# A two-layer decoder trunk on one core: neighbouring blocks paired in both MLPs, the passages into and out of their up-projections reordered, and the down projections' weight halves made by two engines

## Chip, core and metric

The kernel runs on one core of a Trainium2 chip. The metric is the device time of one execution in microseconds, as the median of the runs. The core has TensorE (PE in the rows, with PEld for its weight loads), VectorE (DVE), ScalarE (ACT), GpSimd (POOL), and SyncE (SP), which here only issues DMAs. Each engine takes its own instructions in the order in which they were issued, and they wait for each other by semaphores.

## The reference

The input x is 1024 positions by 1024 channels in float32. There are two layers, each a mixer with a residual and then an MLP with a residual:

```python
for layer in range(2):
    x = x + pool_diffattn_layer(x, ...)   # layer 0; layer 1: mlstm_layer(x, ...)
    x = x + conv_ffn(x, ffn_norm_g[layer], ffn_w_up[layer], ffn_conv_w[layer],
                     ffn_conv_b[layer], ffn_w_down[layer])

def conv_ffn(x, norm_g, w_up, conv_w, conv_b, w_down):
    h = causal_depthwise_conv(rms_norm(x, norm_g) @ w_up, conv_w, conv_b)   # width 3
    g, u = jnp.split(h, 2, axis=-1)                                         # 2816 columns each
    return (jax.nn.silu(g) * u) @ w_down
```

The mixers end in a 1024 by 1024 output projection. The change touches the passage from it into the MLP, the MLP, and nothing else.

## The kernel before

**Precision and layout.** Activations lie transposed: `res[:, c, :]` holds channels 128c to 128c+127 (chunk c of KC = 8) by S = 1024 positions. Each float32 factor is split into a high part (rounded to float32r by a copy) and a low part (the rest); a product is three matmuls: high by high, high by low, low by high. A matmul has 128 by 128 weights and 512 moving columns (HALF).

**Output projection (`pe_out`).** Output chunk d is one weight tile and 8 groups (`pe_group`) of 6 matmuls. It fills one half of PSUM `pj`, the halves alternating. `dve_out_add` adds it into `res`. The last two chunks, 6 and 7, are interleaved after the table `LAST_PAIR`, so that the mixer's input buffer falls free early: in the order 6, 6, 7, 7, 6, 7, five groups of 6, five groups of 7. Each further group of chunk 7 adds one to `xa_free`.

**Up-projection.** It is a Strassen-like product: for each of FC = 22 column blocks j, seven products `a11 s2 s3 s1 a22 a12 s4` (for j = 0 in the order `a11 s1 a12 s4 s2 s3 a22`) of 12 matmuls each. Its moving side is, for each pair of chunks p, the plain first half (`a11`) and the difference of halves (`s1`, made by `dve_out_low` through `wsum`) of one chunk, the whole of the other (`a12`, `s4`), and three sums of both (`s2`, `s3`, `a22`; made from the base copy `rbc` of `act_pair_base` by `dve_pair_sums`, split by `act_pair_high` and `dve_pair_low`). Chunk p is paired with chunk p + 4. The weights are summed by GpSimd (`pool_s1` to `pool_s4`), their high parts cut by ScalarE (`act_cut`, in the order of the products), their low parts made by GpSimd (`pool_low`).

**After the products.** `act_p1` copies `a11`'s result out of PSUM, and `a12` may overwrite that bank only then. VectorE combines (`dve_u2`, `u3`, `c22`, `c21`, `c11`, `c12`); inside `dve_c21` and `dve_c12` it multiplies by the row norm (this gives `ffn_hg` and `ffn_hu`). ScalarE starts the convolution in PSUM `dn` (`act_center`), VectorE adds the two other taps (`dve_taps`), ScalarE does SiLU (`act_silu`), VectorE the gating (`dve_gated`). Product `a22` of block j needs `u3` of the same block, since both use one bank. Gated blocks go to DRAM and come back as `act_stage`.

**Norm statistics.** `act_norm_square` squares each chunk, GpSimd adds (`add_squares`), and `pe_stat` sums across partitions between the products of j = 0.

**Down projection (`pe_down`).** There are 22 weight tiles and 22 activation blocks, in six groups of 4, 4, 4, 4, 2, 4. Block p is split by `act_gated_high` and `dve_gated_low`. The first group starts as each of its first four blocks arrives. Output block 0 needs part `c21` of j = 21, block 1 `c12`, block 2 the last SiLU, block 3 the last gated block. The weight tiles are split by GpSimd alone, high part and low part (`pool_cut`, in the rows L1978 and L1980).

The order of the work on each engine is written out by hand in `act_out_norm`, `dve_out`, `dve_ffn`, `act_ffn`, `pool_ffn` and `sp_ffn`.

## Time and profile before

| | |
|---|---|
| time, median of 3 runs | 2207.36 us (2207.21 to 2207.53) |
| profiled execution: its own time | 2207.0 us |
| its span in the trace | 2204.8 us |
| PE busy | 98% of the span |
| DVE / POOL / ACT busy | 60% / 53% / 36% |
| layer 0: last matmul of the output projection to the first of the up-projection | 404 us |
| layer 0: up-projection / down projection | 404 to 849 / 850 to 1094 us |
| layer 1: up-projection / down projection | 1511 to 1955 / 1956 to 2202 us |

The profiled execution took 0.4 us less than the median of the runs. A row's first number is the start, or the busy time, as its group says; "idle before <- X" is how long the engine stood still before the instruction and what ended that. "issue" is a wait that the profile gives to no instruction, often one for several semaphores. A busy PE isn't PE at its peak: neighbouring matmuls overlap, and one starts every 0.23 us though a row gives 0.39 us.

### The profile page before, as it was taken

What the parts mean: (1) busy time and instruction counts of PE and PEld (TensorE: products, weight loads), DVE (VectorE), ACT (ScalarE), POOL (GpSimd) and SP (SyncE); (2) the same over time, 40 slices, a digit from 0 to 9 for tenths busy, and PEclk for the clock granted to TensorE, in tenths of its full rate; (3) what the DMA queues carried; (4) which work ended last, traced back from release to release, by engine and by line L of the source; (5) the groups of instructions that cost most, each with busy time, mean ns of one, the idle gap of its engine ahead of it and who ended that gap; (6) DMA issues with size and microseconds to landing.
All of it is one profiled execution on the core that took longest, in us unless ns stands there. A gap on an engine that the chain in (4) does not pass through costs nothing.

```text
span 2204.8 us, 26660 instructions
## 1 busy us (share of the span) xinstructions
PE 2153.2 (98%) x10219; PEld 1776.0 (81%) x10219; DVE 1328.5 (60%) x1423; ACT 790.2 (36%) x1266; POOL 1179.4 (53%) x708
## 2 busy tenths in 40 slices
PE   9999999799999999999999999997999999999999
PEld 8777778678888887888888898886788888878887
DVE  7776766677777777334544244366677777773342
ACT  6555452444434443000343434424434444430000
POOL 2212216677777775444643333275777777754442
PEclk9999999899999999999999999998999999999999
DMA  6111012022222224222321021030222222243221
GB/s 204 55 49 49 26 46 107 19 77 87 80 83 77 86 87 153 90 91 71 112 82 58 20 77 58 20 143 19 73 81 79 85 86 87 81 144 100 86 67 77
DMA packets 50429, 174.80 MB, mean 79 GB/s; under 512 B 6080, under 2 KB 8192, under 8 KB 50304
## 3 DMA queue, kind: packets, MB, share of 16 engines
q1 hardware_dynamic: 42816, 147.49, 20.2%
q10 hardware_dynamic: 7488, 25.61, 3.2%
q8 instruction: 82, 1.34, 0.2%
q14 instruction: 43, 0.35, 0.1%
HBM read 139.23 MB, written 29.66 MB: 77 GB/s over the span
## 4 chain that ended last, share of the span: by engine, by line
PE 90%; DVE 5%; issue 3%; POOL 2%; ACT 1%; ACTq 0%; DVEq 0%; POOLq 0%
PE pj L1684 36%; PE pj L355 14%; PE dn L1726 11%; PE pj L1726 10%; PE pj L328 6%; PE pj L2231 3%; PE dn L720 1%; PE pj L746 1%; DVE act_lo_buf L1813 1%; POOL ssum L438 1%; PE dn L2370 1%; PE pj L537 1%; PE pj L730 1%; POOL w_lo L1615 1%; PE dn L2379 1%
## 5 line engine op out<-in xcount | busy, mean ns | idle before, releaser
L1978 POOL TENSOR_TENSOR w_hi<-w_raw,ones 128x1024 fp32r<-128x1024 f32 x98 | 190.4, 1943 | 746.9 <-PE pj L328 170.3
L1615 POOL TENSOR_TENSOR w_lo<-w_sum,w_hi 128x512 fp32r<-128x512 f32 x176 | 272.3, 1559 | 122.6 <-ACT w_hi L1609 122.6
L1980 POOL TENSOR_TENSOR w_lo<-w_raw,w_hi 128x1024 fp32r<-128x1024 f32 x98 | 259.0, 2643 | 7.7
L1609 ACT ACTIVATE w_hi<-w_sum 128x512 fp32r<-128x512 f32 x176 | 106.5, 628 | 311.2 <-POOL w_sum L1630 168.9
L1615 POOL TENSOR_TENSOR w_lo<-w_raw,w_hi 128x512 fp32r<-128x512 f32 x132 | 172.6, 1308 | 81.7 <-ACT w_hi L1609 81.7
L1684 PE MATMUL pj<-t_hi,w_hi 128*128 128x512 f32 x520 | 204.7, 394 | 10.0 <-DVE ffn_v L1759 10.0
L1684 PE MATMUL pj<-t_lo,w_hi 128*128 128x512 f32 x520 | 204.2, 393 | 0.0
L1684 PE MATMUL pj<-t_hi,w_lo 128*128 128x512 f32 x520 | 203.8, 392 | 0.0
L1684 PE MATMUL pj<-xb_hi,w_hi 128*128 128x512 f32 x348 | 136.5, 392 | 12.4 <-issue 12.4
L1684 PE MATMUL pj<-xa_hi,w_hi 128*128 128x512 f32 x348 | 136.2, 391 | 12.4 <-issue 12.4
L1850 ACT ACTIVATE act_hi_buf<-act_stage 128x1024 fp32r<-128x1024 f32 x40 | 41.7, 1056 | 293.1 <-PE dn L1726 192.3
L1870 DVE TENSOR_TENSOR res<-dn,res 128x1024 f32<-128x1024 f32 (+1 forms) x49 | 58.9, 1202 | 134.6 <-PE dn L1726 134.6
L1870 DVE TENSOR_TENSOR res<-pj,res 128x1024 f32<-128x1024 f32 x48 | 58.7, 1224 | 134.6 <-PE pj L1726 134.6
L1684 PE MATMUL pj<-xb_lo,w_hi 128*128 128x512 f32 x348 | 136.3, 392 | 0.0
L1684 PE MATMUL pj<-xb_hi,w_lo 128*128 128x512 f32 x348 | 136.2, 392 | 0.0
L1684 PE MATMUL pj<-xa_lo,w_hi 128*128 128x512 f32 x348 | 136.1, 391 | 0.0
L1684 PE MATMUL pj<-xa_hi,w_lo 128*128 128x512 f32 x348 | 136.0, 391 | 0.0
L355 PE MATMUL pj<-xb_hi,w_hi 128*128 128x512 f32 x384 | 128.3, 415 | 0.0
L1684 PEld LDWEIGHTS pj<-t_hi,w_hi 128*128 128x128 f32 x520 | 98.5, 189 | 35.6 <-issue 10.9
L1609 ACT ACTIVATE w_hi<-w_raw 128x512 fp32r<-128x512 f32 x132 | 82.7, 627 | 103.4 <-PE pj L1684 103.4
L355 PE MATMUL pj<-xb_lo,w_hi 128*128 128x512 f32 x384 | 119.1, 392 | 0.0
L1726 PE MATMUL pj<-act_hi_buf,w_hi 128*128 128x512 f32 x352 | 109.4, 392 | 9.7 <-DVE act_lo_buf L1813 6.2
(378 smaller groups left out, 5459.1 us busy)
## 6 DMA issues: line engine op xcount, KB each, us to landing
w_raw<-weights SPq DMA_DIRECT2D x187, 512.0 KB, 3.5
gated_rows<-ffn_gated SPq DMA_DIRECT2D x40, 512.0 KB, 2.6
act_stage<-gated_rows ACTq DMA_DIRECT2D x32, 512.0 KB, 3.3
x_first<-x_t SPq DMA_DIRECT2D x8, 512.0 KB, 7.5
res<-x_t SPq DMA_DIRECT2D x8, 512.0 KB, 6.7
act_stage<-gated_rows SPq DMA_DIRECT2D x8, 512.0 KB, 5.0
scratch<-res ACTq DMA_DIRECT2D x8, 512.0 KB, 2.6
res<-scratch SPq DMA_DIRECT2D x8, 512.0 KB, 7.3
```

The costliest lines, as they stand in the source:

```text
L328: ins = pe.matmul(o, w, x[:, k, t * HALF:(t + 1) * HALF], start=(k == 0 and m == 0), stop=(k == KC - 1 and m == 2))
L355: ins = pe.matmul(o[:, t * HALF:(t + 1) * HALF], w, x[:, k, t * HALF:(t + 1) * HALF], start=(first and m == 0), stop=(last and m == 2))
L438: eng.tensor_tensor(ssum[:, :], ssum[:, :], squares_of(ph, c)[:, :], ALU.add).then_inc(norm_acc[ph], 1)
L1609: act.activation(f.cut(t, whi), f.source(j, name), ACT.Copy).then_inc(c_high, 1)
L1615: pool.tensor_tensor(f.cut(t, wlo), f.source(j, name), f.cut(t, whi).bitcast(F32), ALU.subtract).then_inc(c_ready, 1)
L1684: ins = pe.matmul(o, f.cut(t, w)[:, k * P:(k + 1) * P], f.moving(name, x, k), start=(not more and k == 0 and q == 0), stop=(k == KC // 2 - ...
L1726: ins = pe.matmul(f.room(e)[:, t * HALF:(t + 1) * HALF], w[:, wsl, at0:at0 + P], x[:, p % SLOTS, t * HALF:(t + 1) * HALF], start=(i == 0 a ...
L1850: act.activation(f.hi[:, p % SLOTS, :], f.gated_source(p), ACT.Copy).then_inc(act_hi, 1)
L1870: dve.tensor_tensor(res[:, d, half], f.room(e)[:, half], res[:, d, half], ALU.add).then_inc(down_added, 1)
L1978: pool.tensor_tensor(whi[:, w, :], raw[:, r, :], ones[:, 0:1].to_broadcast([P, D]), ALU.mult).then_inc(w_high, 1)
L1980: pool.tensor_tensor(wlo[:, w, :], raw[:, r, :], whi[:, w, :].bitcast(F32), ALU.subtract).then_inc(w_ready, 1)
L2231: ins = pe.matmul(value_bank(h, b), XB[mine][:, x, b * P:(b + 1) * P], theirs[:, wsl, w], start=(t == 0 and k == 0 and q == 0 and b % 2 == 0),
```

## The change

- **Pairing.** Chunk 2p is now paired with chunk 2p + 1. Even chunks give `a11` and `s1`, odd ones `a12` and `s4`. The weights are laid out accordingly on the host.
- **Sums during the output projection.** `dve_pair_sums` of pairs 0 and 1 run after chunks 1 and 3, into spare parts of the near buffer (chunks 6 and 7 of X); pair 2's also go there, only pair 3's in the far buffer. So chunk 6 is written after the low parts of pairs 0 and 1, chunk 7 after pair 2's.
- **`LAST_PAIR`**: chunk 7 gets its group 3 before chunk 6's last four.
- **Queues of the passage.** `act_p1` of j = 0 moves ahead of the last two cuts and the last pair's high part. GpSimd makes `s1`, `s2`, `s3` of j = 0 ahead of the sum of squares.
- **Block 0 to 1.** `dve_u2` and `dve_u3` of j = 1 move ahead of the second taps of j = 0; ScalarE does both `act_center` of j = 0 at once.
- **Last block.** The multiplications by the row norm leave `dve_c21` and `dve_c12`; for j = 21 they run after the low parts of the first four gated blocks. ScalarE makes the four high parts in a row.
- **Down weights.** ScalarE copies the high part (`act_down_high`), GpSimd only the low part (`pool_down_low`), in 22 tiles of each layer.

```diff
         def act_out_norm(act, l):
             for c in range(KC - 2):
                 act_out_chunk(act, f, c)
-            act_pair_base(act, f, 0)
+                if c % 2:
+                    act_pair_base(act, f, c // 2)
             act_cut(act, f, 0)
-            act_pair_base(act, f, 1)
+            act_cut(act, f, 1)
             act_pair_high(act, f, 0)
-            act_cut(act, f, 1)
-            act_pair_base(act, f, 2)
             act_pair_high(act, f, 1)
             act_out_chunk(act, f, KC - 2)
             act_cut(act, f, 2)
+            act_pair_high(act, f, 2)
             act_pair_base(act, f, 3)
-            act_pair_high(act, f, 2)
+            act_cut(act, f, 3)
             act_out_chunk(act, f, KC - 1)
-            act_cut(act, f, 3)
+            act_p1(act, f, 0)
             act_cut(act, f, 4)
+            act_cut(act, f, 5)
             act_pair_high(act, f, 3)
-            act_cut(act, f, 5)
...
         def dve_out(dve, l):
             for d in range(KC - 2):
                 dve_out_add(dve, l, d)
                 dve_out_low(dve, f, d)
-            dve_pair_sums(dve, f, 0)
-            dve_pair_sums(dve, f, 1)
+                if d in (1, 3):
+                    dve_pair_sums(dve, f, d // 2)
             dve_pair_low(dve, f, 0)
+            dve_pair_low(dve, f, 1)
+            dve_pair_sums(dve, f, 2)
             dve_out_add(dve, l, KC - 2)
-            dve_pair_low(dve, f, 1)
             dve_out_low(dve, f, KC - 2)
-            dve_pair_sums(dve, f, 2)
+            dve_pair_low(dve, f, 2)
             dve_out_add(dve, l, KC - 1)
-            dve_pair_low(dve, f, 2)
+            dve_pair_sums(dve, f, 3)
             dve_out_low(dve, f, KC - 1)
-            dve_pair_sums(dve, f, 3)
             dve_pair_low(dve, f, 3)
...
+        def act_down_high(act, f, n):
+            if n < f.T1 + W_RING:
+                act.wait_ge(prod_done, f.l * N_PROD * FC + N_PROD * FC - 4 + 2 * (n - f.T1))
+            else:
+                act.wait_ge(tile_done, td(n - W_RING + 1))
+            raw_landed(act, n)
+            act.activation(whi[:, n % W_RING, :], raw[:, n % RAW_RING, :], ACT.Copy).then_inc(w_high, 1)
+        def pool_down_low(pool, n):
+            pool.wait_ge(w_high, td(n + 1))
+            pool.tensor_tensor(wlo[:, n % W_RING, :], raw[:, n % RAW_RING, :], whi[:, n % W_RING, :].bitcast(F32),
+                               ALU.subtract).then_inc(w_ready, 1)
...
             for p in range(4, FC):
                 act_gated_high(act, f, p)
                 act_next_stage(act, f, p)
+                act_down_high(act, f, f.T1 + p - 1)
+            act_down_high(act, f, f.T1 + FC - 1)
```

Three places of the queues follow. Before and after each is layer 0.

ScalarE, the passage into the up-projection, before: `xb_hi` is chunk 7's high part, `t_hi` the last pair's, `ffn_v_0` is `act_p1`, `w_hi` are cuts.

```order
L413 ACTIVATE xb_hi<-res,params 128x1024
L426 ACTIVATE sq_tmp<-res 128x1024
L1609 ACTIVATE w_hi<-w_sum_118 128x512
L1609 ACTIVATE w_hi<-w_sum_119 128x512
L1395 ACTIVATE t_hi_122<-t_sums_124 128x1536
L1609 ACTIVATE w_hi<-w_sum_120 128x512
L1819 ACTIVATE ffn_v_0_126<-pj 128x512
L1609 ACTIVATE w_hi<-w_raw 128x512
```

The same place on ScalarE in the change:

```order
L1631 ACTIVATE w_hi<-w_sum_118 128x512
L413 ACTIVATE xb_hi<-res,params 128x1024
L426 ACTIVATE sq_tmp<-res 128x1024
L1845 ACTIVATE ffn_v_0_130<-pj 128x512
L1631 ACTIVATE w_hi<-w_sum_119 128x512
L1631 ACTIVATE w_hi<-w_sum_120 128x512
L1402 ACTIVATE t_hi_122<-t_sums_last_124 128x1536
L1631 ACTIVATE w_hi<-w_raw 128x512
```

`act_p1` stands right behind chunk 7's square instead of behind the last pair, and the cut of `s4` (source `w_sum_118`) stands ahead of chunk 7.

VectorE, end of block j = 0 and start of j = 1, before: `ffn_v_0` is `u2`, `ffn_v_1` is `u3`, `dn` are taps, `ffn_gated` the gating.

```order
L1800 SCALAR_TENSOR_TENSOR dn<-ffn_hg_125,params,dn 128x1022
L1802 SCALAR_TENSOR_TENSOR dn<-ffn_hg_125,params,dn 128x1023
L1800 SCALAR_TENSOR_TENSOR dn<-ffn_hu_128,params,dn 128x1022
L1802 SCALAR_TENSOR_TENSOR dn<-ffn_hu_128,params,dn 128x1023
L1809 TENSOR_TENSOR ffn_gated_0_130<-ffn_silu_129,dn 128x1024
L1754 TENSOR_TENSOR ffn_v_0_126<-pj,ffn_v_0_126 128x512
L1759 TENSOR_TENSOR ffn_v_1_127<-pj,ffn_v_0_126 128x512
L1767 TENSOR_TENSOR ffn_hg_125<-pj,ffn_v_1_127 128x512
```

The same place on VectorE in the change:

```order
L1826 SCALAR_TENSOR_TENSOR dn<-ffn_hg_129,params,dn 128x1022
L1828 SCALAR_TENSOR_TENSOR dn<-ffn_hg_129,params,dn 128x1023
L1776 TENSOR_TENSOR ffn_v_0_130<-pj,ffn_v_0_130 128x512
L1781 TENSOR_TENSOR ffn_v_1_131<-pj,ffn_v_0_130 128x512
L1826 SCALAR_TENSOR_TENSOR dn<-ffn_hu_132,params,dn 128x1022
L1828 SCALAR_TENSOR_TENSOR dn<-ffn_hu_132,params,dn 128x1023
L1835 TENSOR_TENSOR ffn_gated_0_134<-ffn_silu_133,dn 128x1024
L1789 TENSOR_TENSOR ffn_hg_129<-pj,ffn_v_1_131 128x512
```

`u2` and `u3` have passed the second pair of taps and the gating.

VectorE, the last block j = 21, before: `act_lo_buf` are the low parts of gated blocks for the down projection.

```order
L1776 TENSOR_TENSOR ffn_hg_125<-ffn_hg_125,rms_bc 128x1024
L1813 TENSOR_TENSOR act_lo_buf_133<-ffn_gated_0_130,act_hi_buf_132 128x1024
L1785 TENSOR_TENSOR ffn_hu_128<-pj,rms_bc 128x512
L1813 TENSOR_TENSOR act_lo_buf_133<-act_stage_134,act_hi_buf_132 128x1024
L1789 TENSOR_TENSOR ffn_hu_128<-pj,ffn_v_0_126 128x512
L1794 TENSOR_TENSOR ffn_hu_128<-ffn_hu_128,rms_bc 128x512
L1813 TENSOR_TENSOR act_lo_buf_133<-act_stage_134,act_hi_buf_132 128x1024
L1800 SCALAR_TENSOR_TENSOR dn<-ffn_hg_125,params,dn 128x1022
L1802 SCALAR_TENSOR_TENSOR dn<-ffn_hg_125,params,dn 128x1023
L1813 TENSOR_TENSOR act_lo_buf_133<-act_stage_134,act_hi_buf_132 128x1024
```

The same place on VectorE in the change:

```order
L1839 TENSOR_TENSOR act_lo_buf_137<-ffn_gated_0_134,act_hi_buf_136 128x1024
L1809 TENSOR_TENSOR ffn_hu_132<-pj,rms_bc 128x512
L1839 TENSOR_TENSOR act_lo_buf_137<-act_stage_138,act_hi_buf_136 128x1024
L1813 TENSOR_TENSOR ffn_hu_132<-pj,ffn_v_0_130 128x512
L1839 TENSOR_TENSOR act_lo_buf_137<-act_stage_138,act_hi_buf_136 128x1024 x2
L1800 TENSOR_TENSOR ffn_hg_129<-ffn_hg_129,rms_bc 128x1024
L1820 TENSOR_TENSOR ffn_hu_132<-ffn_hu_132,rms_bc 128x512
L1826 SCALAR_TENSOR_TENSOR dn<-ffn_hg_129,params,dn 128x1022
```

The four low parts now stand ahead of both multiplications by `rms_bc` and ahead of the taps.

## Rows read from the trace of the kernel before

**Rows 1.** Page, busy time, share of the span and instructions of each engine.

```profile
PE 2153.2 (98%) x10219; PEld 1776.0 (81%) x10219; DVE 1328.5 (60%) x1423; ACT 790.2 (36%) x1266; POOL 1179.4 (53%) x708
```

**Rows 2.** Waits of PE: line, for whom, us in total, times, longest us.

```profile
PE pj L1684 <- issue: 24.9, 2, 12.4
PE pj L1684 <- DVE ffn_v L1759: 10.0, 2, 5.0
PE pj L1726 <- DVE act_lo_buf L1813: 6.2, 4, 2.0
PE pj L1726 <- issue: 3.5, 2, 1.8
```

**Rows 3.** Windows: length, PE, PEld, DVE, ACT, POOL busy, PEclk, DMA share, GB/s.

```profile
422.00:428.00 6.00, 5.85 (x15) 4.66 (x16) 0.84 (x1) 0.57 (x2) 3.21 (x2) 0.57 0.27 83
...
1969.00:1975.00 6.00, 6.00 (x21) 4.74 (x20) 5.87 (x5) 2.01 (x2) 2.05 (x2) 0.72 0.35 130
...
876.00:1093.00 217.00, 217.00 (x959) 179.72 (x959) 89.31 (x66) 28.58 (x28) 100.98 (x43) 1.00 0.28 94
```

**Rows 4.** Timeline of PE, layer 0, blocks 0 and 1: start, us, idle before.

```profile
422.15 0.77 PE L1684 MATMUL pj<-xb_hi,w_hi 128*128 128x512 f32 x1 [12.43 <-issue]
...
427.32 0.39 PE L1684 MATMUL dn<-xb_hi,w_hi 128*128 128x512 f32 x1
...
430.04 1.95 PE L373 MATMUL dn<-ones,ssum 128*128 128x128 f32 x16
...
456.98 0.76 PE L1684 MATMUL pj<-t_hi,w_hi 128*128 128x512 f32 x1 [5.02 <-DVE ffn_v L1759]
```

**Rows 5.** Timeline of ACT in the same stretch.

```profile
419.56 1.48 ACT L1395 ACTIVATE t_hi<-t_sums 128x1536 fp32r<-128x1536 f32 x1 [6.08 <-DVE t_sums L1456]
...
421.47 0.58 ACT L1819 ACTIVATE ffn_v<-pj 128x512 f32<-128x512 f32 x1
...
446.55 1.28 ACT L1834 ACT_TABLE_LOAD   x1
...
451.41 0.58 ACT L1819 ACTIVATE ffn_v<-pj 128x512 f32<-128x512 f32 x1
```

**Rows 6.** Timeline of POOL: sums of squares, and one low part of weights.

```profile
386.06 2.62 POOL L438 TENSOR_TENSOR ssum<-ssum,sq_tmp 128x1024 f32<-128x1024 f32 x1 [6.64 <-ACT sq_tmp L426]
...
401.63 3.37 POOL L438 TENSOR_TENSOR ssum<-ssum,sq_tmp 128x1024 f32<-128x1024 f32 x1
...
434.22 1.28 POOL L1615 TENSOR_TENSOR w_lo<-w_raw,w_hi 128x512 fp32r<-128x512 f32 x1 [9.01 <-ACT w_hi L1609]
```

**Rows 7.** Timeline of DVE: pair sums, chunk 6 added, pair sums again.

```profile
392.56 0.74 DVE L1451 SCALAR_TENSOR_TENSOR t_sums<-res,params,rms_bc 128x512 f32<-128x512 f32 x1
...
397.58 1.23 DVE L1423 TENSOR_TENSOR res<-pj,res 128x1024 f32<-128x1024 f32 x1 [1.10 <-PE pj L355]
...
402.67 2.88 DVE L1451 SCALAR_TENSOR_TENSOR t_sums<-res,params,rms_bc 128x512 f32<-128x512 f32 x1
```

**Rows 8.** Timeline of PE at the start of layer 0's down projection.

```profile
853.26 0.70 PE L1726 MATMUL pj<-act_hi_buf,w_hi 128*128 128x512 f32 x2 [1.76 <-issue]
...
862.32 0.73 PE L1726 MATMUL pj<-act_hi_buf,w_hi 128*128 128x512 f32 x2 [1.97 <-DVE act_lo_buf L1813]
```

**Rows 9.** Timeline of DVE there: two low parts of gated blocks.

```profile
846.31 3.42 DVE L1813 TENSOR_TENSOR act_lo_buf<-ffn_gated,act_hi_buf 128x1024 fp32r<-128x1024 f32 x1
...
855.27 1.21 DVE L1813 TENSOR_TENSOR act_lo_buf<-act_stage,act_hi_buf 128x1024 fp32r<-128x1024 f32 x1
```

**Rows 10.** Timeline of POOL there: a low part of down weights.

```profile
845.38 3.26 POOL L1980 TENSOR_TENSOR w_lo<-w_raw,w_hi 128x1024 fp32r<-128x1024 f32 x1
```

**Rows 11.** Page, groups: busy us, mean ns of one, idle before.

```profile
L1615 POOL TENSOR_TENSOR w_lo<-w_sum,w_hi 128x512 fp32r<-128x512 f32 x176 | 272.3, 1559 | 122.6 <-ACT w_hi L1609 122.6
L1980 POOL TENSOR_TENSOR w_lo<-w_raw,w_hi 128x1024 fp32r<-128x1024 f32 x98 | 259.0, 2643 | 7.7
...
L1850 ACT ACTIVATE act_hi_buf<-act_stage 128x1024 fp32r<-128x1024 f32 x40 | 41.7, 1056 | 293.1 <-PE dn L1726 192.3
```

167 lines of the change are left out of this document (103 added, 64 removed).

## The prediction

> **What bounds the kernel now.** First the page's busy times: PE is busy for 98% of the span, the others for 60% or less [rows 1]. So time can only come from PE's gaps, or from matmuls at a lower clock. The list of PE's waits shows where the gaps are [rows 2]: 24.9 us in two waits at L1684 (products, 12.4 us in each layer), 10.0 us in two at L1684 for `u3` (5.0 each), and 6.2 + 3.5 = 9.7 us in six waits at L1726, the start of the down projections. All else PE waits for is under 4 us. In the timeline of PE the first is product `a12` of block 0, the second `a22` of block 1 [rows 4]; the third are the first matmuls of the down projection [rows 8]. The steady part of the down projection has no gap (217.0 of 217.0 us busy [rows 3]), so a cheaper weight cut gains nothing there.
>
> **Clock.** Behind the two longer gaps matmuls are slow. In the steady window 959 start in 217.0 us, one per 0.226 us, at a granted clock of 1.00 (the 2.4 GHz level). The 12 matmuls of `a12` take 427.32 - 422.15 = 5.17 us instead of 2.72: that is the 1.2 GHz level for all of it (the window's mean is 0.57) [rows 3, 4], 2.4 us lost. I allow 1.8 us for `a22`, which starts after 5.02 us of idling. After the shorter gaps of the down projection (2.0 us at most) the clock stayed up in layer 0, but in layer 1 it fell: 0.72 in a window of 6.0 us, (1 - 0.72) x 6.0 = 1.7 us [rows 2, 3].
>
> **First gap, block 0.** `a12` waits for three things: its weights, chunk 7 of X, and `act_p1`. The profile names none ("issue"). `act_p1` ends at 421.47 + 0.58 = 422.05 and `a12` starts at 422.15, so it is `act_p1`. It stands behind the last pair's high part, which itself had waited 6.08 us for VectorE's sums [rows 4, 5]. The change puts it behind chunk 7's square. What is then late? I follow the new queue in the clock of layer 0.
>
> - Chunk 6 now ends one group later. A group is 6 x 0.226 = 1.36 us, so its add (397.58 [rows 7]) starts at 398.94 and ends at 400.17. Difference, high halves and square on ScalarE and VectorE take about 2.4 us more: square done at 402.6.
> - GpSimd then makes sum of squares, low part of `a12`, and `s4`. Alone that is 2.62 + 1.28 + 1.28 = 5.2 us, beside a busy VectorE 3.37 + 1.56 + 1.56 = 6.5 us [rows 6, 11], with a row of the worst some 1 us more. ScalarE has now the cut of `s4` ahead of chunk 7, so this wait holds chunk 7 up: cut done 408.4 to 410.1.
> - Chunk 7's high part, its square and `act_p1` follow, 1.1 + 1.0 + 0.6 = 2.7 us with the starts overlapping a little [rows 5, 11]. `a12` starts between 411.2 and 412.9. I take 412.2, in the upper half, since VectorE works on `pair_low` and sums then. PE began the last of `s1` 12.6 us before 422.15, near 409.6 (its idle time and one step of 0.23), so a gap of 2.6 us remains instead of 12.4.
> - Its last three matmuls need chunk 7's low part. VectorE has ahead of it the sums of pair 3: three instructions at 0.74 alone, up to 2.88 beside GpSimd [rows 7]. That puts the low part at 411.8 to 417.4; I take 415.4, some 1.3 us of further gap.
> - `a12` then ends at 416.1, `s4` at 418.8 (416.6 to 420.8). Before, `s4` ended at 430.04 [rows 4]. Gain 11.2 us (9.2 to 13.4), the slow matmuls' 2.4 us included.
> - Will the clock fall after 2.6 + 1.3 us? Between cases that did (5.0, 12.4) and one layer of two that did at 2.0. I take half of 2.4: **gain 10.0 us in each layer**, bounds 6.8 and 13.4.
>
> Pair sums 0 and 1 now run during the output projection. VectorE has 10.9 us per chunk there and gets some 8 us for an even chunk and 10 for an odd one. PSUM alternates, so it may be a whole chunk late before PE waits: cost nothing. It would cost something from an average of 10.9 us.
>
> **Second gap, block 1.** `u3` of block 1 stood behind the second taps and the gating, and ended just before it. Now it stands before them, but `u2` needs `act_p1` of block 1, which ScalarE makes behind `act_silu`, and that needs the first taps and its table (load at 446.55, 1.28 us). One `act_center` more (1.2 us) now precedes the load and one fewer follows. `act_p1` moves only from 451.41 to 450.8 [rows 5]; then 0.6 + 0.7 + 0.7 us and `a22` can start at 453.0 instead of 456.98 [rows 4]: 4.0 us, and the 1.8 us of slow matmuls with it, as 1.2 us of idling remain. But VectorE has the taps and the gating still to do (3.9 us) and so begins block 1's `c21` 1.7 us late. Its round has little slack (in the last block `u3` ended 0.3 us before PE wanted it; the timeline there is not among the rows), so `a22` of block 2 waits 0.9 to 1.5 us. **Gain 4.6 us in each layer**, bounds 2.3 (clock still falls) and 5.8 (no wait in block 2).
>
> **Third gap, start of the down projection.** There VectorE's four low parts stood among a multiplication, taps, and waits for ScalarE. Now they come first, each followed only by the combination that frees a PSUM bank. Times here are again layer 0's, from the timeline of that stretch, of which the rows give the ends. Block 0's high part is ready at 844.45 as before, the others at 1.06 us each [rows 11], with a down weight's high part of 1.06 us in between: 846.5, 847.5, 848.5. The low parts end near 845.8, 849.4, 851.3 and 852.5, and `c12` at 850.1. PE finishes the products at 848.6 and uses a block each 2.7 us: only 0.2 us is left to wait, or 0.7 if the first low part takes 3.42 us as in [rows 9]. What is late next is the last SiLU, which output block 2 needs at 859.7: multiplication 1.3, centre 1.2, taps 2.6, SiLU 1.0, so ready at 858.8, 0.9 us before; beside GpSimd the multiplication alone takes 1 us more. I leave 0.4 us. Gain 9.7 / 2 - 0.4 = 4.5 in layer 0, and 4.5 + 1.3 = 5.8 in layer 1 where the clock had fallen: **10.3 us in both**, bounds 5 and 12.
>
> A page of the Trainium skill bears on this, "SBUF — State Buffer", section "Who interferes with whom": a VectorE instruction with two SBUF inputs and a GpSimd one that reads SBUF lock each other out whole, and the later one waits. The row agrees: the low part of 3.42 us began inside GpSimd's, which ended at 848.64, and ended 1.1 us after that, where another took 1.21 us [rows 9, 10]. By that rule the first low part, at 844.5 now ahead of GpSimd's start at 845.6, takes 1.2 us and the gain is 0.5 us per layer more than by the row of 3.42.
>
> **Down weights on ScalarE.** 44 copies of 1.06 us on an engine busy for 36% [rows 1, 11], GpSimd keeps its 2.64 us. Behind each copy ScalarE queues the next gated block's high part. A copy may start when tile n - 3 is done, and its 1.1 + 2.6 us lie under two tiles of 10.9 us each. Cost nothing; if the cover went, 3.7 us per tile at most.
>
> **Sum.** 2 x 10.0 + 2 x 4.6 + 10.3 = 39.5 us. The profiled execution would go from 2207.0 to 2167.5 us (span 2165.3, with 2.2 us around it). The median is 0.4 us above it: **2167.9 us**, 1.8% faster. With all lower bounds, 2 x 6.8 + 2 x 2.3 + 5 = 23.2 us, 2184; with all upper ones 2 x 13.4 + 2 x 5.8 + 12 = 50.4 us, 2157.
>
> **Rivals.**
>
> - *The work is in a cheaper order than I draw it*: no clock fall after the first gap, chunk 7's low part early, no wait in block 2. Then 2 x 12.5 + 2 x 5.8 + 11 = 47.6 us, 2160. For it: many of my durations are those beside GpSimd. Against: GpSimd is busy just then.
> - *The gap moves to chunk 7's chain*: GpSimd's sum of squares, `s4`, the cut, chunk 7, `act_p1` are one chain now, and the clock falls at both places. Gain 2 x 7 + 2 x 2.8 + 8 = 27.6 us, 2180. For it: every step there has a row that is longer under contention [rows 6, 7].
> - *Slower: ScalarE's queue in the down projections.* A weight's copy stands behind a gated-block DMA issue that waits for VectorE's low part, which waits for PE's output block. If it came so late that the tile's low part ended after PE was done with the tile before, PE would stop once per tile. It decides from 18 us of delay, 21.8 - 3.7. At 2 us in each of 19 tiles of two layers: +76 - 39.5, 2244. Against: by my reading VectorE's low part p + 1 comes before the tile's end for which the copy waits anyway.
> - *It does nothing*: `a12` really waited for chunk 7 or weights. Then only the other gaps go, 20 us, 2187. Against: the end of `act_p1` and the start of `a12` meet within 0.1 us [rows 4, 5], and in both layers alike [rows 2].
>
> **Chances.** Forecast (31 to 45 us) 0.60; cheaper order 0.15; moved gap (22 to 31 us) 0.13; `act_p1` not the cause 0.03; slower 0.04; something small that cancels nearly all 0.02, the rest between these. About 0.2% (4.4 us) is what a measurement of this kernel can tell from no change. Faster 0.94, same 0.02, slower 0.04. The range, 2157 to 2182, leaves out the slower case and the ends of the others.
>
> **What will show it.** `a12`'s idle at 2 to 4 us instead of 12.4, its releaser `act_p1` or chunk 7's low part; `s4` ended 11 us sooner after the output projection. `a22` of block 1 idle for 1 us, with a wait of 1 us in block 2. The six waits at L1726 nearly gone. POOL's busy time down by its 44 copies, ACT's up by 44 x 1.06 = 47 us, PE's window of the down projection unchanged. I am wrong if the output projection shows gaps, if PE waits at each weight tile, or if the clock's slow matmuls take over what the gaps gave.

## The result, and the profile after

The changed kernel takes **2169.16 us** (median of 4 runs, 2168.22 to 2173.05) against 2207.28 us for the kernel before on the same chip: the ratio is 0.9831, with a 95% interval from 0.9814 to 0.9848. The forecast was 2167.9 us. The profiled execution took 2168.6 us.

The page, busy times of the engines, to be read against [rows 1]:

```profile
span 2166.8 us, 26682 instructions
...
PE 2146.3 (99%) x10219; PEld 1771.1 (82%) x10219; DVE 1330.1 (61%) x1425; ACT 832.1 (38%) x1312; POOL 1075.4 (50%) x664
```

PE has the same 10219 matmuls and is busy 7 us less, since fewer of them run at the lower clock. POOL lost its 44 instructions and 104 us, ACT has 46 more and 42 us. The span fell by 2204.8 - 2166.8 = 38.0 us.

The waits of PE in the kernel after (line, for whom, us in total, times, longest us), against [rows 2]:

```profile
PE pj L1706 <- DVE ffn_v L1781: 7.6, 4, 2.5
PE pj L1706 <- POOL w_lo L1637: 2.6, 1, 2.6
PE pj L1706 <- issue: 2.6, 1, 2.6
```

L1706 is the products' line now, L1748 that of the down projection. Nothing waits at L1748 any more, where there were six waits. The first gap is 2.6 us in each layer instead of 12.4 (the profile gives it to "issue" in one layer and to a low part of weights in the other), and two waits for `u3` in each layer stand where there was one. The timeline of PE, layer 0:

```profile
412.70 0.76 PE L1706 MATMUL pj<-xb_hi,w_hi 128*128 128x512 f32 x1 [2.59 <-issue]
...
417.06 0.40 PE L1706 MATMUL dn<-xb_hi,w_hi 128*128 128x512 f32 x1
...
419.80 1.95 PE L373 MATMUL dn<-ones,ssum 128*128 128x128 f32 x16
...
442.96 0.47 PE L1706 MATMUL pj<-t_hi,w_hi 128*128 128x512 f32 x1 [1.23 <-DVE ffn_v L1781]
...
464.79 0.47 PE L1706 MATMUL pj<-t_hi,w_hi 128*128 128x512 f32 x1 [2.54 <-DVE ffn_v L1781]
...
835.60 0.62 PE L1748 MATMUL pj<-act_hi_buf,w_hi 128*128 128x512 f32 x2
```

These are `a12` and `s4` of block 0, the statistic, `a22` of block 1, `a22` of block 2, and the first matmul of the down projection. Two stretches make comparison easy. **U** runs from the first product's first matmul to the first one of the down projection. Before it took 445.77 us in layer 0 and 444.67 in layer 1, after it 431.09 and 430.92. **M** runs from the start of the first down projection to the first product of layer 1: 661.56 us before, 657.50 after.

On ScalarE the row that the forecast was about, and three rows of block 1 that matter below (timeline of ACT, kernel after):

```profile
409.51 0.63 ACT L1631 ACTIVATE w_hi<-w_sum 128x512 fp32r<-128x512 f32 x1 [3.47 <-POOL w_sum L1664]
...
412.03 0.58 ACT L1845 ACTIVATE ffn_v<-pj 128x512 f32<-128x512 f32 x1
...
450.43 1.16 ACT L1631 ACTIVATE w_hi<-w_sum 128x512 fp32r<-128x512 f32 x2 [3.70 <-POOL w_sum L1659]
451.49 0.61 ACT L1631 ACTIVATE w_hi<-w_raw 128x512 fp32r<-128x512 f32 x1
452.01 1.19 ACT L1854 ACTIVATE dn<-ffn_hg,params 128x1024 f32<-128x1024 f32 x1
```

`act_p1` (L1845) ends at 412.61, and `a12` starts at 412.70. What holds `act_p1` back is the cut of `s4` at 409.51, which waited 3.47 us for GpSimd's sum, with chunk 7's high part and square between.

### The profile page after: what moved, and what is told of

The parts are those of the page before. It is cut to its first block and busy times, and to the rows that moved or that the text cites. A ratio compares the mean times of both kernels' runs of the same rounds, so it can differ in the third digit from the quotient of the medians.

```text
span 2166.8 us, 26682 instructions
## 1 busy us (share of the span) xinstructions
PE 2146.3 (99%) x10219; PEld 1771.1 (82%) x10219; DVE 1330.1 (61%) x1425; ACT 832.1 (38%) x1312; POOL 1075.4 (50%) x664
## 5 line engine op out<-in xcount | busy, mean ns | idle before, releaser
L2039 POOL TENSOR_TENSOR w_hi<-w_raw,ones 128x1024 fp32r<-128x1024 f32 x54 | 105.8, 1959 | 494.3 <-PE pj L328 170.3
L1637 POOL TENSOR_TENSOR w_lo<-w_sum,w_hi 128x512 fp32r<-128x512 f32 x176 | 274.2, 1570 | 103.0 <-ACT w_hi L1631 103.0
L1896 POOL TENSOR_TENSOR w_lo<-w_raw,w_hi 128x1024 fp32r<-128x1024 f32 x44 | 105.9, 2407 | 342.1 <-ACT w_hi L1891 342.1
L1706 PE MATMUL pj<-t_hi,w_hi 128*128 128x512 f32 x520 | 203.1, 391 | 7.6 <-DVE ffn_v L1781 7.6
L1637 POOL TENSOR_TENSOR w_lo<-w_raw,w_hi 128x512 fp32r<-128x512 f32 x132 | 172.7, 1309 | 64.1 <-ACT w_hi L1631 64.1
L1706 PE MATMUL pj<-t_hi,w_lo 128*128 128x512 f32 x520 | 202.8, 390 | 0.0
L1706 PE MATMUL pj<-t_lo,w_hi 128*128 128x512 f32 x520 | 202.7, 390 | 0.0
L1891 ACT ACTIVATE w_hi<-w_raw 128x1024 fp32r<-128x1024 f32 x44 | 46.6, 1059 | 317.6 <-PE dn L1748 168.7
L1706 PE MATMUL pj<-xb_hi,w_hi 128*128 128x512 f32 x348 | 136.3, 392 | 2.6 <-issue 2.6
L1706 PE MATMUL pj<-xa_hi,w_hi 128*128 128x512 f32 x348 | 136.2, 391 | 2.6 <-POOL w_lo L1637 2.6
L2041 POOL TENSOR_TENSOR w_lo<-w_raw,w_hi 128x1024 fp32r<-128x1024 f32 x54 | 135.1, 2502 | 4.2
L1706 PE MATMUL pj<-xa_lo,w_hi 128*128 128x512 f32 x348 | 136.1, 391 | 0.0
L1706 PE MATMUL pj<-xa_hi,w_lo 128*128 128x512 f32 x348 | 135.9, 391 | 0.0
L1706 PE MATMUL pj<-xb_lo,w_hi 128*128 128x512 f32 x348 | 135.9, 391 | 0.0
L1706 PE MATMUL pj<-xb_hi,w_lo 128*128 128x512 f32 x348 | 135.9, 391 | 0.0
L1839 DVE TENSOR_TENSOR act_lo_buf<-act_stage,act_hi_buf 128x1024 fp32r<-128x1024 f32 x40 | 80.2, 2008 | 80.0 <-ACT act_hi_buf L1876 80.0
L1706 PEld LDWEIGHTS pj<-t_hi,w_hi 128*128 128x128 f32 x520 | 97.6, 188 | 33.5 <-issue 6.3
L355 PE MATMUL pj<-xb_hi,w_lo 128*128 128x512 f32 x384 | 118.5, 390 | 0.0
```

The source lines that it names most:

```text
L355: ins = pe.matmul(o[:, t * HALF:(t + 1) * HALF], w, x[:, k, t * HALF:(t + 1) * HALF], start=(first and m == 0), stop=(last and m == 2))
L1637: pool.tensor_tensor(f.cut(t, wlo), f.source(j, name), f.cut(t, whi).bitcast(F32), ALU.subtract).then_inc(c_ready, 1)
L1706: ins = pe.matmul(o, f.cut(t, w)[:, k * P:(k + 1) * P], f.moving(name, x, k), start=(not more and k == 0 and q == 0), stop=(k == KC // 2 - ...
L1839: dve.tensor_tensor(f.lo[:, p % SLOTS, :], f.gated_source(p), f.hi[:, p % SLOTS, :].bitcast(F32), ALU.subtract).then_inc(act_lo, 1)
L1891: act.activation(whi[:, n % W_RING, :], raw[:, n % RAW_RING, :], ACT.Copy).then_inc(w_high, 1)
L1896: pool.tensor_tensor(wlo[:, n % W_RING, :], raw[:, n % RAW_RING, :], whi[:, n % W_RING, :].bitcast(F32), ALU.subtract).then_inc(w_ready, 1)
```

## The experiments

Each time is compared with runs of the kernel before on the same chip (their medians lie between 2206.36 and 2207.49 us). Five of the runs split the change's gain, seven look for what is left.

### The first gap: `act_p1` put back (x1_p1_back)

```diff
 # act_out_norm of the kernel after
             act_out_chunk(act, f, KC - 1)
-            act_p1(act, f, 0)
             act_cut(act, f, 4)
             act_cut(act, f, 5)
             act_pair_high(act, f, 3)
+            act_p1(act, f, 0)
```

> The changed kernel with act_p1 of block 0 moved back behind the last cuts and the last pair's high part; all else as changed. Theory A (act_p1 frees the bank and its place in ScalarE's queue sets when a12 starts): the last high part ends at 415.0 in the changed trace, so act_p1 ends near 416.1 and a12 starts 3.4 us later in each layer (idle about 6 us instead of 2.6, matmuls behind it slow again), 2169 + 7 = 2176 us. Rival (chunk 7's low part, ready at 416.2, sets it anyway): the gap grows, but a12's last three matmuls waited until then already, so less than 2 us in all.

Measured: 2175.45 us (2175.13 to 2176.21), ratio 0.9857 [0.9842, 0.9872]. Waits of PE in this kernel:

```profile
PE pj L1706 <- issue: 10.0, 2, 5.0
PE pj L1706 <- DVE ffn_v L1781: 7.5, 4, 2.5
```

One instruction behind three others costs 6.3 us. The gap is 5.0 us and not the 6 expected, since `act_p1` ends at 414.81; `a12` starts at 414.91, 0.1 us behind it, as it does in the kernels before and after. The block waits don't move.

### The first gap: only `act_p1` moved, in the kernel before (x2_p1_on_before)

```diff
 # kernel before: act_out_norm
             act_out_chunk(act, f, KC - 1)
+            act_p1(act, f, 0)
             act_cut(act, f, 3)
 # act_ffn
-            act_p1(act, f, 0)
             act_cut(act, f, 2 * W_RING)
```

> The kernel before with one edit: act_p1 of block 0 stands right behind chunk 7's square. Pairing, sums and all other orders as before. Theory A (the first gap was mostly the queue position of act_p1): a12 starts when chunk 7's low part is there, 413.5 instead of 422.15 in layer 0's clock, and the last pair's low part (422.8) is then just in time for s2's last matmuls: 8.7 + up to 2.4 us of slow matmuls per layer, 2207 - 17 to 22 = 2185 to 2190 us. Rival (the pairing and the sums during the output projection carry the first gap's 10.6 us): the wait moves to s2, whose sums are as late as before, and less than 10 us are won in all, 2197 us or more.

Measured: 2188.53 us (2188.05 to 2189.76), ratio 0.9917 [0.9902, 0.9931]. Waits of PE:

```profile
PE pj L1685 <- DVE ffn_v L1760: 10.0, 2, 5.0
PE pj L1685 <- issue: 6.7, 2, 3.3
PE pj L1727 <- DVE act_lo_buf L1814: 6.2, 4, 2.0
PE pj L1727 <- issue: 3.5, 2, 1.8
```

This moved line alone gives 19 us, half of the whole change. The gap falls from 12.4 to 3.3 us, where the whole change has 2.6; the other waits stay as in [rows 2]. From the first product to the statistic it is 16.1 and 17.2 us in the two layers, 15.3 and 15.4 in the kernel after: so the rest of the passage's changes (the pairing with its sums during the output projection, `LAST_PAIR`, the order of the other work) is worth 0.8 and 1.8 us on top, and part of the 1.8 is the clock, as layer 1 of this run has 14 slow matmuls behind the gap and layer 0 has 9. The rest pays in another way: with the old position of `act_p1` the new kernel waits 5.0 us where the old one waited 12.4. No run takes the pairing apart from the other orders.

### The first gap: `act_p1` still earlier (x10_passage)

```diff
 # kernel after: act_out_norm
+            act_p1(act, f, 0)
             act_cut(act, f, 3)
             act_out_chunk(act, f, KC - 1)
-            act_p1(act, f, 0)
 # dve_out
-            dve_pair_sums(dve, f, 3)
             dve_out_low(dve, f, KC - 1)
+            dve_pair_sums(dve, f, 3)
```

> After, with ScalarE's reading of the first block's product ahead of the cut of its last weight, and VectorE's last low part of the normalised input ahead of the last pair of sums. If the 2.6 us left at the first gap are ScalarE standing behind that cut (which waited 3.47 us for GpSimd's sum), the gap at 412.7 falls to 0 to 0.5 us in each layer, 4 to 5 us in all; if the clock then does not fall, another 1.5 us a layer comes with it: 2161 to 2165 us. If the last sum is late for its weight, a new wait of up to 1.5 us a layer stands behind the low part of the paired input: 2166 to 2168 us.

Measured: 2170.07 us (2168.53 to 2170.25), ratio 0.9833 [0.9820, 0.9846]: no change, and above both expectations. The timeline of PE says where the 2.6 us went:

```profile
412.50 0.47 PE L1706 MATMUL pj<-xb_hi,w_hi 128*128 128x512 f32 x1 [0.60 <-DVE xb_lo L1450]
421.90 0.50 PE L1706 MATMUL pj<-t_hi,w_hi 128*128 128x512 f32 x1 [1.92 <-DVE t_lo L1476]
```

`a12` now starts with no gap and only its last three matmuls wait 0.6 us. But the last pair's sums begin 2.9 us later on VectorE and their low part is late for `s2`, 1.9 us in each layer: the risk named beforehand. From the first product to the statistic this kernel takes 11.7 us, 3.6 less than the kernel after, and all of it is lost again behind the statistic. Block 1's wait rose too in layer 0 (2.10 us; it is 0.71 in layer 1). So the cause of the gap is right, and this cure hands it on.

### The third gap: only the weights' high parts on ScalarE (x4_weights_on_before)

```diff
 # kernel before: act_ffn, pool_ffn
+                act_down_high(act, f, f.T1 + p - 1)
...
-                pool_cut(pool, n, n, 16 * (n // RAW_RING + 1))
+                pool_down_low(pool, n)
```

> The kernel before with ScalarE making the high parts of the down weights and GpSimd the low parts, nothing else changed. Theory A: the first low part is no longer held for 3.4 us behind GpSimd's, so 0 to 4 us in all are won, all at the start of the down projections, and the other waits there (for the last low part behind the taps) stay: 2203 to 2207 us. Rival (ScalarE's queue becomes late in the steady part): waits at each tile, above 2207 us.

Measured: 2204.23 us (2202.87 to 2205.47), ratio 0.9986 [0.9976, 0.9995]. Waits of PE at the down projection:

```profile
PE pj L1726 <- DVE act_lo_buf L1813: 4.5, 2, 2.3
PE pj L1726 <- issue: 0.8, 2, 0.4
```

5.3 us of waits instead of 9.7, so 4.4 us less. Of these 1.2 us come back as slow matmuls, since the clock now falls behind the last wait in layer 0, where it had stayed up (0.83 from 856 to 866 us, against 1.00 from 858 to 868 in the kernel before). ScalarE's 44 copies cost nothing that shows, and GpSimd's 102 us less of work bring 3 us.

### The third gap: the weights back on GpSimd (x3_weights_back)

The same edit undone in the kernel after.

> The changed kernel with the down projections' weights split by GpSimd alone again, both parts. Theory A (the steady down projection has no gap, the cheaper cut gains only at its start, where GpSimd's longer work locks VectorE out of its low parts): 0.3 to 3 us per layer slower, in waits at the start of the down projections, steady part unchanged: 2170 to 2175 us. Rival (the start is carried by VectorE's new order alone): within 1 us of the changed kernel.

Measured: 2177.35 us (2174.92 to 2178.58), ratio 0.9864 [0.9849, 0.9879]: 8.2 us, more than expected. Timeline of PE in this kernel, then of DVE, then of POOL:

```profile
848.78 0.98 PE L1748 MATMUL dn<-act_hi_buf,w_hi 128*128 128x512 f32 x2 [1.86 <-issue]
```

```profile
836.96 5.64 DVE L1839 TENSOR_TENSOR act_lo_buf<-act_stage,act_hi_buf 128x1024 fp32r<-128x1024 f32 x2
842.53 1.21 DVE L1800 TENSOR_TENSOR ffn_hg<-ffn_hg,rms_bc 128x1024 f32<-128x1024 f32 x1
```

```profile
835.55 2.64 POOL L2032 TENSOR_TENSOR w_hi<-w_raw,ones 128x1024 fp32r<-128x1024 f32 x1 [0.20 <-PE pj L1706]
838.27 3.26 POOL L2034 TENSOR_TENSOR w_lo<-w_raw,w_hi 128x1024 fp32r<-128x1024 f32 x1
```

And the same place in the kernel after (timeline of DVE):

```profile
831.51 1.23 DVE L1839 TENSOR_TENSOR act_lo_buf<-ffn_gated,act_hi_buf 128x1024 fp32r<-128x1024 f32 x1 [0.46 <-ACT act_hi_buf L1876]
...
836.61 2.34 DVE L1839 TENSOR_TENSOR act_lo_buf<-act_stage,act_hi_buf 128x1024 fp32r<-128x1024 f32 x2
```

Two low parts take 5.64 us beside GpSimd's two instructions and 2.34 us when GpSimd rests. The 3.3 us go through the multiplication, the centre term and the taps into the last SiLU, which output block 2 awaits: 1.86 us of wait, and the first matmuls behind it are slow (0.98 us for two, 0.62 else). M grows by 661.78 - 657.50 = 4.3 us, of which this wait is 1.9, a shorter one at the start 0.3, and the slow matmuls, by the starts of their rows, 1.7. So in waits the move is worth the same in both orders, 4.4 us in the old one and 2 x (1.86 + 0.3) = 4.3 in the new one. In time it is worth 3 us in the old order and 8 in the new one, and the difference is the clock: here each layer's long wait brings slow matmuls that the kernel after has none of, while in the old order the move leaves waits of 2.3 us and their slow matmuls in place.

### The third gap: the last block's old order (x8_last_back)

```diff
 # kernel after: dve_ffn, last block
             dve_c21(dve, f, j)
+            dve_hg(dve, f, j)
             dve_gated_low(dve, f, 0)
             dve_c11(dve, f, j)
             dve_gated_low(dve, f, 1)
             dve_c12(dve, f, j)
+            dve_hu(dve, f, j)
             dve_gated_low(dve, f, 2)
-            dve_gated_low(dve, f, 3)
-            dve_hg(dve, f, j)
-            dve_hu(dve, f, j)
             dve_taps(dve, f, j, 0)
+            dve_gated_low(dve, f, 3)
             dve_taps(dve, f, j, 1)
 # act_ffn: the centre term between the high parts again
```

> After, with the last block's order on VectorE and ScalarE as it was before (multiplication of the gate half ahead of the low parts, centre term between the high parts), and the high parts of the down weights left on ScalarE. If the order carries the rest of the third gap, PE waits again at the start of the down projection as in the run with the weights alone, 2.3 to 2.7 us a layer, and with slow matmuls behind it 5 to 7 us in all: 2174 to 2176 us. If moving the weights' high parts was enough once the rest of the kernel is changed: 2169 us.

Measured: 2176.27 us (2176.07 to 2176.99), ratio 0.9860 [0.9843, 0.9876]. The waits at L1748 are 4.5 and 0.8 us, the very numbers of the run with the weights alone:

```profile
PE pj L1748 <- DVE act_lo_buf L1839: 4.5, 2, 2.3
PE pj L1748 <- issue: 0.8, 2, 0.4
```

The third gap was 9.7 us of waits. The weights take away 4.4, the order the other 5.3. The time grew by more, 7.1 us; 2.2 us of it lie in U of layer 0 (433.3 us against 431.1), where the clock also fell behind block 2's wait in the profiled execution, far from the edit.

### Block 2's wait: GpSimd sooner (x6_cut_first)

```diff
 # kernel after: act_ffn
             act_cut(act, f, 2 * W_RING)
+            act_cut(act, f, N_PROD)
             act_stat_factors(act, ph)
-            act_cut(act, f, N_PROD)
```

> After, with the high part of the normalised input's last chunk made ahead of the statistic's factors on ScalarE, so that GpSimd can begin block 1's sums some 2.7 us sooner (it idled 2.68 us for this high part at 423.98). GpSimd theory (block 2's first matmul waits 2.54 us because GpSimd is late with the sums that ScalarE's block 1 cuts need): that wait falls to 0 to 0.5 us in each layer, 2164 to 2165 us. VectorE theory (VectorE's own work of block 1 is too long, as the prediction had it): the wait stays 2.5 us, 2169 us. ScalarE's queue order theory: the wait shrinks only by as much as the cuts come sooner.

Measured: 2170.89 us (2167.8 to 2171.2), ratio 0.9835 [0.9822, 0.9849], and block 2's wait is 2.51 us in both layers. GpSimd does begin block 1's sums 3.2 us sooner (422.01 instead of 425.22), but 18 us later only 0.5 us of that are left (440.33, against 440.81): it waits again for ScalarE's cuts. Its late start isn't the cause. In layer 0 the clock stayed up behind the first gap here, and chunk 7's low part now holds up `a12` (timeline of PE):

```profile
415.82 0.47 PE L1706 MATMUL pj<-xb_hi,w_hi 128*128 128x512 f32 x1 [1.05 <-DVE xb_lo L1450]
```

### Block 2's wait: the first centre term ahead of the cuts (x7_center_first)

```diff
 # kernel after: act_ffn, j = 1
+                    if j == 1 and i == 4:
+                        act_center(act, f, j, 0)
...
                     if i == 6:
-                        if j < FC - 1:
+                        if 1 < j < FC - 1:
                             act_center(act, f, j, 0)
```

> After, with the centre term of block 1's first half put on ScalarE ahead of the last cuts of block 2's sums instead of behind them. ScalarE's queue theory (the centre term at 452.0 stood behind cuts that waited 3.70 us for GpSimd's sum, and VectorE's taps waited 3.45 us for it): block 2's wait of 2.54 us goes to 0 to 0.3 us in each layer, with everything else in place, 2164 to 2165 us. VectorE theory: the wait stays at 2.5 us, 2169 us; if the cuts that now come later are themselves needed at once, a new wait of up to 1.2 us a layer stands on the low or high part of a weight.

Measured: 2169.84 us (2169.02 to 2171.93), ratio 0.9835 [0.9821, 0.9848]: no gain, and block 2's wait is 3.0 us instead of 2.5. Timeline of ACT, then of DVE:

```profile
448.77 1.21 ACT L1854 ACTIVATE dn<-ffn_hg,params 128x1024 f32<-128x1024 f32 x1 [2.49 <-DVE ffn_hg L1800]
...
457.56 0.63 ACT L1631 ACTIVATE w_hi<-w_sum 128x512 fp32r<-128x512 f32 x1 [3.87 <-POOL w_sum L1664]
458.10 1.19 ACT L1854 ACTIVATE dn<-ffn_hu,params 128x1024 f32<-128x1024 f32 x1
459.23 0.58 ACT L1845 ACTIVATE ffn_v<-pj 128x512 f32<-128x512 f32 x1
```

```profile
450.01 1.29 DVE L1826 SCALAR_TENSOR_TENSOR dn<-ffn_hg,params,dn 128x1022 f32<-128x1022 f32 x1 [0.68 <-ACT dn L1854]
...
459.32 1.29 DVE L1826 SCALAR_TENSOR_TENSOR dn<-ffn_hu,params,dn 128x1022 f32<-128x1022 f32 x1 [4.26 <-ACT dn L1854]
```

The first centre term came 3.2 us sooner and the first taps with it. VectorE then stood still for 4.26 us, since the second centre term (458.10) was behind the cut of the next `s4`, which waited 3.87 us for GpSimd. The theory of ScalarE's queue was right in kind; I had named one of two places.

### Block 1's wait: its `act_p1` ahead of the SiLU (x9_p1_of_1)

```diff
 # kernel after: act_ffn
                     if i == 0:
+                        if j == 1:
+                            act_p1(act, f, j)
                         act_silu(act, f, j - 1)
                     if i == 1:
                         if j > 1:
                             act_center(act, f, j - 1, 1)
-                        act_p1(act, f, j)
+                            act_p1(act, f, j)
```

> After, with the plain product of block 1 read by ScalarE ahead of block 0's SiLU (and its table load). If block 1's accumulator is held by its first reader on ScalarE, block 1's wait of 1.23 us in each layer goes to 0, and the time falls by 2.5 us to 2166.7 us. If it is held by VectorE's reading of the other accumulator, nothing moves: 2169 us. If the SiLU, later by 0.6 us, holds up block 2, block 2's wait of 2.54 us grows by as much and the sum stays within 1 us of 2169.

Measured: 2170.26 us (2169.57 to 2170.47), ratio 0.9835 [0.9822, 0.9849]. Block 1's wait is gone, but the time isn't better. Block 2's wait is 3.2 us, and slow matmuls follow it (timeline of PE, then of DVE):

```profile
463.86 0.55 PE L1706 MATMUL pj<-t_hi,w_hi 128*128 128x512 f32 x1 [3.23 <-DVE ffn_v L1781]
464.21 0.63 PE L1706 MATMUL pj<-t_lo,w_hi 128*128 128x512 f32 x1
```

```profile
444.35 0.69 DVE L1794 TENSOR_TENSOR ffn_hg<-pj,ffn_v 128x512 f32<-128x512 f32 x1 [0.29 <-PE pj L1706]
...
452.31 1.28 DVE L1826 SCALAR_TENSOR_TENSOR dn<-ffn_hg,params,dn 128x1022 f32<-128x1022 f32 x1 [4.55 <-ACT dn L1854]
```

So the two block waits are largely one delay paid in two places. Counted from the start of `a12`, `a22` of block 2 begins at 51.4 us here and at 52.1 in the kernel after (layer 0): of the 1.2 us won in block 1, 0.7 are left, and the slow matmuls behind the longer wait take those. VectorE isn't late any more at block 1's `c21` (the first row, where it waits for PE), and block 2 waits all the same, because VectorE then stands still for 4.55 us for the centre term.

### All of ScalarE's queue of blocks 1 and 2 (x13_blocks)

The edits of the last two runs together, and for j = 2 the second centre term and `act_p1` ahead of the cut at i = 1:

```diff
+                    if j == 2 and i == 1:
+                        act_center(act, f, 1, 1)
+                        act_p1(act, f, 2)
```

> After, with ScalarE's queue of blocks 1 and 2 rearranged as one piece: block 1's plain product read ahead of block 0's SiLU, block 1's first centre term ahead of the cuts of block 2's sums, and its second centre term and block 2's plain product ahead of the cut that waits for GpSimd's next sum. Each of these alone only handed the wait on (from block 1 to block 2, or from the first centre term to the second). If ScalarE's queue is the whole cause, u3(2) ends about 459.4 us against its matmul at 460.5 and both block waits go to 0, 3.7 us a layer, 7.4 us of PE's waits and about 1 us of slow matmuls behind them: 2161 to 2163 us. If GpSimd's sums are the bound behind it, some 2 us a layer stay as a wait on the low part of a weight: 2165 to 2167 us. If VectorE's work itself is, 2168 to 2170 us.

Measured: 2165.7 us (2164.3 to 2165.96), ratio 0.9811 [0.9796, 0.9826]. No wait in blocks 1 and 2 is left. VectorE's `u3` of block 2 starts at 459.16 and is done before `s1` ends. But block 3 now waits, which none of the three expectations had:

```profile
PE pj L1706 <- DVE ffn_v L1781: 4.1, 2, 2.1
```

7.6 us of waits became 4.1.

### The passage as well (x12_both)

```diff
 # added to the run above; act_out_norm
+            act_p1(act, f, 0)
+            act_norm_high(act, 2 * l + 1, KC - 1, f.X, res[:, KC - 1, :], ready, value)
             act_cut(act, f, 3)
-            act_out_chunk(act, f, KC - 1)
-            act_p1(act, f, 0)
+            act_norm_square(act, 2 * l + 1, KC - 1, res[:, KC - 1, :])
 # dve_out
-            dve_pair_sums(dve, f, 3)
+            dve_pair_sums(dve, f, 3, (0,))
             dve_out_low(dve, f, KC - 1)
+            dve_pair_sums(dve, f, 3, (1, 2))
```

and `act_cut(act, f, N_PROD)` moved as in the run x6_cut_first. `dve_pair_sums` does the steps that its last argument names, `ready` and `value` are the wait of `act_out_chunk`.

> The kernel of the blocks run with the passage rearranged too: ScalarE reads the first block's product, then makes chunk 7's high part, then the cut that waits for GpSimd; VectorE makes chunk 7's low part between the first and the second operation of the last pair sums; and the cut of block 1's plain product stands ahead of the statistic's factors. If the 2.6 us at the first gap are ScalarE's queue alone, they go to 0 to 0.5 us in each layer and the slow matmuls behind them (1.5 us) go too, with up to 1 us a layer of a new wait for the last pair's low part: 2154 to 2159 us. If, as with the simpler rearrangement, the wait is handed on to the last pair's low part (1.9 us a layer) in full, the gain over the blocks run is under 2 us.

Measured: 2161.52 us (2159.24 to 2162.39), ratio 0.9792 [0.9777, 0.9806], 2.5 us above the expected range, as block 3 still waits 2.0 to 2.2 us with slow matmuls behind. The first gap has shrunk to 0.4 us behind the last pair's low part (waits of PE):

```profile
PE pj L1710 <- DVE ffn_v L1785: 4.2, 2, 2.2
...
PE pj L1710 <- DVE t_lo L1479: 0.8, 2, 0.4
```

From the first product to the statistic it is 11.52 us in both layers, 15.3 and 15.4 in the kernel after and 25.9 and 25.3 before.

### Every block (x14_all_blocks)

```diff
 # act_ffn of the run above
-                    if j == 1 and i == 4:
+                    if i == 4 and j < FC - 1:
                         act_center(act, f, j, 0)
-                    if j == 2 and i == 1:
-                        act_center(act, f, 1, 1)
-                        act_p1(act, f, 2)
+                    if i == 1 and j > 1:
+                        act_center(act, f, j - 1, 1)
+                        act_p1(act, f, j)
...
-                    if i == 1 and j > 2:
-                        act_center(act, f, j - 1, 1)
-                        act_p1(act, f, j)
-                    if i == 6:
-                        if 1 < j < FC - 1:
-                            act_center(act, f, j, 0)
```

> The kernel with blocks and passage rearranged, with the order of ScalarE's queue that blocks 1 and 2 have now in every block: the first centre term ahead of the cuts of the next block's sums, the second one and the next plain product ahead of the cut that waits for GpSimd's next sum. In the run before it the wait had moved to block 3 (2.1 to 2.2 us in each layer at 479.03, with 1 us of slow matmuls behind it), where the centre term stood behind cuts again (idle 3.70 on ScalarE, 3.45 on VectorE). If that queue is the cause there too, the wait goes: 2155 to 2158 us. If VectorE and GpSimd lag behind TensorE from the passage on for another reason, the wait goes on to block 4 and the time stays at 2160 to 2162 us. If cuts that now stand behind a centre term are late in the steady blocks, new waits on the low part of a weight make it slower than 2162 us.

Measured: **2154.05 us** (2153.72 to 2154.21), ratio 0.9759 [0.9746, 0.9773], slightly better than the best expectation. It beats both kernels: 15 us below the kernel after, 53 below the one before. Waits of PE at the products, all that is left, and a window (PE busy, then PEld, DVE, ACT, POOL, clock, DMA share, GB/s):

```profile
PE pj L1710 <- DVE t_lo L1479: 0.8, 2, 0.4
```

```profile
430.00:480.00 50.00, 50.00 (x222) 41.31 (x221) 38.70 (x36) 23.98 (x33) 42.57 (x32) 1.00 0.29 95
```

That window was 46.23 us busy in the kernel after. U is 423.64 and 423.83 us, and the mean clock of the execution is 1.000 (0.998 after, 0.991 before). Against the run before it, the 4.2 us of waits gave 7.5 us: by the starts of the rows, the other 3.3 us are slow matmuls that stood behind them.

## Why the prediction came out right, point by point

The time was 1.3 us off, and the sum of 39.5 us stands against 38.0 measured in the span. The terms, with the first gap as the way from the first product to the statistic, the second as the rest of U without its last wait, and the third as that wait (1.11 us) with what lies behind:

| term | forecast, both layers | measured |
|---|---|---|
| first gap | 20.0 | 10.64 + 9.95 = 20.6 |
| second gap | 9.2 | 2.93 + 2.69 = 5.6 |
| third gap | 10.3 | 5.17 + 7.02 = 12.2 |
| output projection of layer 0 | 0 | -0.4 |
| sum | 39.5 | 38.0 |

(Third gap: 1.11 + 661.56 - 657.50, and 1.11 + 5.91, where 5.91 is how much shorter the end of the span is behind the second start. The output projection's -0.4 is scatter: the first product starts between 404.02 and 404.54 us over all the kernels.)

That the sum is nearer than its terms is luck: the errors are +0.6, -3.6, +1.9 and -0.4 us and offset each other.

- **First gap: right, the gap itself by its own working.** Forecast: `a12` at 412.2 with a gap of 2.6 us; it started at 412.70 with 2.59, and 0.4 of the 0.5 us lies in the output projection, which ended later by that. The chain named (GpSimd's sum, the cut of `s4`, chunk 7, `act_p1`) is the one in the rows, and x1 and x2 show that the place of `act_p1` carries it. The last steps are right in their sum only. Chunk 7's low part ended at 416.16, even later than forecast (415.4), and still cost nothing, because the clock fell in both layers: `a12` took 417.06 - 412.70 = 4.36 us for 12 matmuls instead of 2.72, and its last three, which need the low part, came at 416.35 anyway. The forecast added 1.3 us for the wait and 1.2 for half a clock fall, but the slow matmuls run through the wait. Where the clock stayed up behind this gap (layer 1 of x3, layer 0 of x6, layer 1 of x13), PE did wait 1.05 to 1.09 us for that low part, and from the first product to the statistic these take 15.1 us, against 15.3 and 15.4 in the kernel after: here the fall cost 0.2 to 0.3 us net. So the end of `s4`, 419.80 against 418.8 + 1.2 = 420.0, came out right with two wrong parts in it.
- **Second gap: the term that was mis-sized, for a wrong cause.** Block 1 was right (wait 1.23 us, 1.2 forecast, no slow matmuls). Block 2 waited 2.54 us and not 0.9 to 1.5, so 5.6 us came of 9.2: per layer 5.02 - 1.23 - 2.54 = 1.25 us of idling and the slow matmuls behind the old gap. The step that failed is "But VectorE has the taps and the gating still to do (3.9 us) and so begins block 1's `c21` 1.7 us late" as the reason for block 2's wait. The lateness came, but VectorE stood idle behind it for longer, 3.45 us for the centre term at 452.01, which stood behind two cuts that waited for GpSimd (the row below, timeline of DVE). I had worked out VectorE's load and never followed ScalarE's queue through block 1. x13 shows it: with VectorE's work untouched and only ScalarE's order changed, both waits go, and x14 removes block 3's in the same way. That the gain itself comes from `u2` and `u3` standing ahead of the second taps is read from the rows; no run put them back.

```profile
453.23 1.29 DVE L1826 SCALAR_TENSOR_TENSOR dn<-ffn_hg,params,dn 128x1022 f32<-128x1022 f32 x1 [3.45 <-ACT dn L1854]
```

- **Third gap: gone, more than forecast.** The wait of 0.4 us and the late SiLU didn't come (SiLU ended at 845.04, its output block starts near 846.5). The forecast had "0.2 us is left to wait, or 0.7 if the first low part takes 3.42 us as in [rows 9]": it took 1.23 us (831.51 above). This is what the rule of the Trainium skill gave ("SBUF — State Buffer", "Who interferes with whom": a VectorE instruction with two SBUF inputs and a GpSimd one that reads SBUF contend for one pair of ports, which is an exclusive lock). The trace agrees: VectorE's began at 831.51, and GpSimd's only at 832.51. The rows of x3 agree once more: 5.64 us for two low parts, behind and between GpSimd's. The term of layer 1 was also too small by its own rows: the clock's fall there is worked out as 1.7 us ([rows 3]) and then enters the sum as 1.3.
- **Down weights on ScalarE.** "Cost nothing" is right: no gap in the steady projection (216.00 of 216.00 us busy from 860 to 1076), and no wait at a weight tile. The rival of a slower kernel is thereby out. But I counted no gain for it by itself either, only as part of the third gap, and by x3 it carries 8 us there, slow matmuls included. ScalarE's busy time rose by 42 us and not by 47.
- **Rivals.** "It does nothing" fell with x1 and x2. "The gap moves to chunk 7's chain" is true of the place and not of the size. "A cheaper order" needed no clock fall and no wait in block 2, and both came.

What stays open: x10's 2.10 us of block 1's wait in one layer and 0.71 in the other weren't followed up, nor which of the rearrangements in x12 is worth how much of its 4 us, nor what the pairing alone is worth.

## What to carry to other kernels

An in-order engine that serves two chains should be read as a queue, and each instruction that others wait for should stand ahead of the ones that themselves wait: 19 us came of one moved line, and 15 more of ScalarE's order with a split of VectorE's sums. A wait that is handed on isn't a refuted cause: two cures that each gained nothing (x7, x9) gave 3.5 us together with a third place of the same queue, and 7.5 more when every block had it. Where a short gap is left, price it with the matmuls behind it, which often run at half the clock for a while. But don't add that price to a second wait that stands right behind the gap, as this prediction did: the slow matmuls run through it.
